# Where eight rounds of key choice stand in the even layer, and where ten unread products stand

## The reference, cut to what matters

```
rel = jax.nn.relu(jnp.einsum('bqhd,bkd->bqhk', qib, ki).astype(jnp.float32))
score = jnp.einsum('bqhk,bqh->bqk', rel, wib.astype(jnp.float32))
score = jnp.where(causal[None], score, -jnp.inf)
_, idx = lax.top_k(score, topk)                  # topk = 64
...
logits = jnp.einsum('bqhd,bqnhd->bhqn', qb, kg).astype(jnp.float32) * (dh ** -0.5)
prob = jax.nn.softmax(logits, axis=-1)
return jnp.einsum('bhqn,bqnhd->bqhd', prob.astype(vg.dtype), vg)
```

## Time and profile before

| | us |
|---|---|
| median of 3 runs | 2285.63 |
| lowest and highest | 2285.41, 2286.16 |
| profiled execution, its own time | 2282.66 |
| its span in the profile | 2281.4 |
| PE busy | 1956.2 (86% of the span) |
| DVE busy | 929.4 (41%) |
| ACT busy | 685.3 (30%) |

### The profile page before, as it was taken

How to read it: one execution, slowest core, us unless ns; L and a number is a source line. 1 busy time by engine, 2 the same in 40 slices (tenths; PEclk the granted TensorE clock), 3 DMA queues, 4 the chain that set the end, 5 groups by cost and what they waited for, 6 DMA issues and landing times.

```text
span 2281.4 us, 30553 instructions
## 1 busy us (share of the span) xinstructions
PE 1956.2 (86%) x13502; PEld 1391.6 (61%) x13502; DVE 929.4 (41%) x1596; ACT 685.3 (30%) x1090; POOL 4.1 (0%) x11
## 2 busy tenths in 40 slices
PE   7899999889898999999999888888899976566666
PEld 5589999868776999866774332333256843232323
DVE  6766655657665665654441110101065510010101
ACT  5445544553524444434422000000034310000000
POOL 0000000000000000000000000000000000000000
PEclk9999999899999999999999999999999988788878
DMA  7564445341467435412227999999932689999997
GB/s 284 225 258 171 167 146 203 146 180 38 185 236 282 174 133 197 185 40 111 111 111 299 427 428 427 428 428 427 428 129 111 268 356 426 427 427 427 427 427 334
DMA packets 44788, 606.56 MB, mean 266 GB/s; under 512 B 5104, under 2 KB 5232, under 8 KB 6768
## 3 DMA queue, kind: packets, MB, share of 16 engines
q1 hardware_dynamic: 43488, 597.61, 64.4%
q0 software_dynamic: 880, 4.98, 0.7%
q10 hardware_dynamic: 288, 2.02, 0.2%
HBM read 603.54 MB, written 1.05 MB: 265 GB/s over the span
## 4 chain that ended last, share of the span: by engine, by line
PE 53%; DMA 27%; DVE 13%; ACT 6%; issue 2%; SPq 0%; DVEq 0%; ACTq 0%
PE ps L85 52%; DMA m_more<-moe_up 9%; DMA m_ring<-moe_up 5%; DMA m_ring<-moe_down 3%; DVE m_WL L94 2%; DMA m_moe_sc<-moe_gate 2%; DMA m_side_slot<-moe_down 2%; DMA m_more<-moe_down 2%; DMA m_more<-moe_gate 1%; DMA m_ring<-moe_gate 1%; ACT m_WH L91 1%; ACT m_mix_sc L91 1%; DVE m_od_low L100 1%; DMA m_ring<-ev_in 1%; PE ps L88 1%
## 5 line engine op out<-in xcount | busy, mean ns | idle before, releaser
L94 DVE TENSOR_TENSOR m_WL<-m_ring,m_WH 128x1024 fp32r<-128x1024 f32 (+1 forms) x277 | 329.9, 1202 | 263.4 <-ACT m_WH L91 262.6
L85 PE MATMUL ps<-m_more,m_moe_sc 128*32 128x256 f32 (+1 forms) x1648 | 319.5, 540 | 79.4 <-DMA m_more<-moe_up 51.4
L91 ACT ACTIVATE m_WH<-m_ring 128x1024 fp32r<-128x1024 f32 (+1 forms) x277 | 282.4, 1034 | 131.1 <-PE ps L85 119.6
L85 PE MATMUL ps<-m_ring,m_moe_sc 128*32 128x256 f32 (+1 forms) x1104 | 246.9, 551 | 54.9 <-DMA m_ring<-moe_gate 28.2
L85 PEld LDWEIGHTS ps<-m_more,m_moe_sc 128*32 128x32 f32 (+1 forms) x1648 | 120.2, 141 | 226.8 <-issue 115.3
L85 PE MATMUL ps<-m_nH,m_WH 128*128 128x256 f32 x936 | 234.5, 287 | 18.3 <-ACT m_WH L91 18.3
L85 PE MATMUL ps<-m_nL,m_WH 128*128 128x256 f32 x936 | 234.5, 287 | 9.1 <-DVE m_nL L100 9.0
L85 PEld LDWEIGHTS ps<-m_nH,m_WH 128*128 128x128 f32 x936 | 181.0, 193 | 22.0 <-ACT m_WH L91 20.2
L85 PEld LDWEIGHTS ps<-m_nL,m_WH 128*128 128x128 f32 x936 | 180.8, 193 | 12.7 <-DVE m_nL L100 11.9
L85 PEld LDWEIGHTS ps<-m_ring,m_moe_sc 128*32 128x32 f32 (+1 forms) x1104 | 89.4, 143 | 148.8 <-issue 77.6
L91 ACT ACTIVATE m_moe_sc<-ps 32x512 f32<-32x512 f32 (+3 forms) x86 | 40.2, 473 | 386.3 <-PE ps L85 375.0
(11 more groups left out here) (307 smaller groups left out, 3193.1 us busy)
## 6 DMA issues: line engine op xcount, KB each, us to landing
m_more<-moe_up SPq DMA_DIRECT2D x37, 2048.0 KB, 26.7
m_more<-moe_gate SPq DMA_DIRECT2D x33, 2048.0 KB, 26.7
m_more<-moe_down SPq DMA_DIRECT2D x29, 2048.0 KB, 23.4
m_ring<-moe_gate SPq DMA_DIRECT2D x26, 2048.0 KB, 24.9
m_ring<-moe_down SPq DMA_DIRECT2D x25, 2048.0 KB, 26.7
m_ring<-ada SPq DMA_DIRECT2D x24, 2048.0 KB, 7.5
m_ring<-moe_up SPq DMA_DIRECT2D x22, 2048.0 KB, 25.5
m_ring<-ffn_down SPq DMA_DIRECT2D x16, 1408.0 KB, 6.0
```

What stands on the lines that cost most here:

```text
L85: return Issued() if self.dry else self.e.matmul(out, lhsT, rhs, start=start, stop=stop, skip_group_check=skip)
L91: return Issued() if self.dry else self.e.activation(*a, **k)
L94: return Issued() if self.dry else self.e.tensor_tensor(*a)
```

## The change

All eight rounds of `pick` come behind "k turned" and `fill(2)`; the four that stood ahead of `until(jobs[1])` are gone from there. On PE the first run of unread products shrinks from 10 to 4, and the second grows from 4 to 7. ACT's and SP's lists are the same.

```
             pe_jobs.until(jobs[1])
             pe_jobs.fill(1)
-            pe_warm(10)
+            pe_warm(4)
             for t in range(2):
                 pe_transposes(("qT", t), block4(eq, t), ["q turned"], fg, ("qT out", t))
...
                 if i == 0:
-                    pe_warm(4)
+                    pe_warm(7)
                 ps, before = fg.take(("PV", i), ("mL", 4 + i))
...
-            pick(4)
             dve_jobs.until(jobs[1])
...
             dve_jobs.fill(2)
-            pick(4)
+            pick(8)
             dve.wait_ge(*V.now()).tensor_scalar(bias, score, TAKEN, 1.0, ALU.is_equal, ALU.subtract).then_inc(*V.mark())
```

## The result

The changed kernel is slower. Its median is 2292.1 us (2289.67 to 2293.79, 8 runs) beside 2284.18 us (2279.21 to 2288.73, 8 runs) for the kernel before in the same comparison. The ratio is 1.0034 with a 95% interval of 1.0025 to 1.0043: 7.8 us more, 5.7 to 9.8. The forecast was 2293.0 us, 7.4 us more than the 2285.63 us that the three runs known then had as their median.

A forecast was written before the change was run, and what follows sets the result against it. The chain was taken to run through DVE's second four rounds and a load, then PE from 111.39. Terms 0 + 5.75 + 1.36 + 0.3 = +7.4 us on 2285.63 gave 2293.0 us, range 2290.3 to 2296.0.

The forecast's parts named there:

- part 1: Four rounds leave DVE's first place, ahead of the low parts at 68.75: hidden behind a load, gain 0.
- part 2: Four rounds added on DVE behind the second four push back bias, last low part of `v` and load: +5.75 us.
- part 3: Unread products on PE: shorter first run gains 0, longer second run delays products with `v` by +1.36 us.
- part 4: Low PE clock behind two widened waits, ahead of `q`'s transposes and the last low part of `v`: +0.3 us.
- The bound of 1.9 us: Upper bound for the clock's cost on PE: two low-clock stretches, 3.1 - 1.16 us.
- The sum: Whole kernel: 0 + 5.75 + 1.36 + 0.3 = +7.4 us, with nothing behind giving it back.
- (a): Added unread products on PE are covered, only the moved rounds count: 2291.4 us; chance 0.08.
- (b): First four rounds on DVE were on the path too: 2287.0 us, not slower 0.08; stronger form to 2281, faster 0.03.
- (c): Delay is taken up later, where the kernel waits for loads: 2286 to 2288 us; chance 0.06.
- (d): Low clock hits PE's second run of unread products: 2298.0 us if all hit, 2294.5 to 2296 for one stretch; chance 0.09.
- The times named as marks: Times expected in the profile after: mean square of `q` 71.8, load 100.75, products with `v` 118.5 to 119.2.

The follow-up runs named there:

- without the first rounds: Kernel before with the first four rounds left out entirely; 48.7 us from mask to products with `v` against 48.8, whole time ratio 0.9999.
- rounds only: Kernel before with all eight rounds behind the rotation of keys, unread products kept at 10 and 4; 54.8 us mask to products with `v`, ratio 1.0031.
- low part early in the changed kernel: Changed kernel with the last low part of `v` formed behind the second of the eight rounds; 56.4 us mask to products with `v`, ratio 1.0034.
- products only: Kernel before with unread products at 4 and 7, rounds where they were; 50.5 us mask to products with `v`, ratio 1.0004.
- low part early: Kernel before with the last low part of `v` formed between second and third of the second four rounds; 46.8 us mask to products with `v`, ratio 0.9999.
- warm start: Kernel before with 8 unread products on PE at the very start; 48.6 us mask to products with `v`, ratio 0.9999.
- without second rounds: Kernel before with the second four rounds left out entirely; 46.6 us mask to products with `v`, ratio 0.9994.
- spread: Kernel before with one second-place round ahead of `k`'s mean square, `v`'s last low part behind the next, second unread run 2; 46.0 us mask to products, ratio 0.9986.
- wait filled: Changed rounds with 10 and 7 unread products, and 7 more ahead of the rest of `v`; 56.3 us mask to products with `v`, ratio 1.0040.
- spread with warm start: Kernel before with one round moved ahead, `v`'s last low part earlier, second unread run 2, and 8 unread products at the start; 45.3 us, ratio 0.9993.

## Why the prediction was right

**The first place (part 1)** was right: a gain of 0 was taken, and DVE's 5.48 us of idle time and the kernel without the first rounds show it.

**The second place (part 2)** was right: 5.75 us by the rounds, 6.0 at the products with `v` in "rounds only". The sentence that the load can't hide it was true, but it was only half the reason. With the load out of the way (the low part early in the changed kernel) the softmax on DVE was as late.

**The unread products (part 3)** were right: 1.36 us forecast, 1.6 at the place in "products only". Fourteen matmuls took 6.20 us in the changed kernel, 2.48 more than eight, and the wait ahead of the products with `v` was used up.

**PE's clock (part 4)** was mis-sized. Taken: 0.3 us, from one stretch of 3.40 us that loses 1.55, of which 1.16 are covered. In the changed kernel the granted clock was 0.50 from 104 to 108 and 0.66 on average from 108 to 111, so low for about 4 + 2 = 6 us. From the low products to the transposes of the probabilities PE needed 113.61 - 104.41 = 9.20 us, against 101.64 - 95.03 = 6.61 before: 2.6 us lost, not 1.55. Of these 1.2 us came through at `zc`: 114.24 - 75.41 = 38.8 us behind the mean square of `q`, against 31.9 before and 5.75 for the rounds. The bound of 1.9 us held. The rule of the Trainium skill ("TensorE: Matmul & The Clock Gate", "HAM oscillation — how this bites in real kernels"), that each burst behind a long wait starts cold, was borne out at both widened waits, 0.50 behind each; the forecast gave it less weight than it had. Behind the first wait it cost nothing, as forecast: the transposes of `k` start 14.03 us behind the mean square of `q` in both kernels (89.44 and 75.41 after), and only PE's wait ahead of them is gone, which was 2.18 us:

```profile
85.81 1.09 PE L88 MATMUL ps<-m_small,m_ev 128*128 128x128 f32 x8 [2.18 <-DVE m_ev L94]
```

**The sum** was 7.4 us. In the changed kernel the first piece of `zc` comes 5.75 + 1.2 us later behind the mean square of `q`, and from there to the products with `v` it is 123.32 - 114.24 = 9.08 us against 7.71 before, 1.4 more: together 8.3, which is what the place shows (47.9 against 39.6). The end shows 7.8 (5.7 to 9.8) and can't tell 7.4 from 8.3, so the mis-sized clock doesn't show in it. Rivals (a), (b) and (c) are out by the experiments. Rival (d), the low clock in the second run of unread products, didn't come true: that run took 6.20 us. In the changed kernel with the low part early the low clock came nearer to that run (0.50 from 106.6 to 112), but it cost its 2.7 us ahead of it, and the run took 6.20 us there too.

**The times named as marks** (mean square at 71.8, load at 100.75, products with `v` at 118.5 to 119.2) were wrong by 3.6 us and the clock's 1.2 at most, since they took the start of the program as fixed. It isn't.

## What to carry to other kernels

Put optional work of an engine where it waits for a load, and take it from where the chain runs: four rounds were free at one place and cost their full length at the other, with one engine and one list. What is freed in the other direction is less, because another engine's own list is late next. A wait that grows on PE can cost twice where no room follows it, once as the wait and once as slow work behind it; and if a kernel's executions differ by more than the change, measure from a mark inside the trace that lies ahead of the change.

## What the runs showed of the hardware

The start of the program took from 62.6 to 69.4 us up to the same instruction, the mask on the score, in twelve profiles of kernels that are the same up to there except for the unread products at the start in two of them. The larger part of the difference is PE's low clock at the start, which ends at a different moment in each execution (15.16 us against 18.77 for the same 71 matmuls). Between the shortest and the longest (18.92, with the low part early) that is 3.8 us. The rest is a second stretch of low clock, between about 49 and 56 us, in four of the twelve (rounds only, products only, without second rounds, low part early), which have the four latest masks. It follows a wait of 1.83 us on PE that is there in all twelve. In the chain, before and with the low part early:

```profile
45.78 2.13 PE ps L85 x8
```

```profile
49.89 3.78 PE ps L85 x8
```

These 8 matmuls and the 56 behind them in the chain take 10.16 us before and 12.91 with the low part early. With the 3.76 us of the 71 matmuls that is 6.5 of the 6.85 us by which the mask is later there. In the stretches of the kernels before and after the granted clock is given as 1.00 there, though the matmuls are slow; the trace has no record of the clock that early. There the length of equal matmuls is the better witness: products of 512 columns took 0.63 us where the clock was given as 0.50 (20.2 to 27 us with the warm start) and 0.39 where it was 1.00, and in the changed kernel they take 0.63 us until 27.7 us, in the kernel before 0.40 from 22.5 us on.

A wait of 2.2 to 2.6 us on PE, ahead of the transposes of `k` and some 7 us behind one of 0.8 to 1.1 us, is there in nine of the twelve profiles. It was followed by the low clock in six (rounds only, both without four rounds, low part early, spread, warm start) and not in three (before, wait filled, spread with warm start). So the profile from which the forecast was made had the rarer case there. It didn't matter for the time: without the first rounds and with the warm start the low stretch was there, and the products with `v` came as in the kernel before (39.6 us), since the wait ahead of the first piece of `zc` covered it. The six waits of 4.8 to 6.4 us (two after, one with the rounds alone, one with the products alone, two in the changed kernel with the low part early) were each followed by it.
